# Gated DeltaNet heads in chunks of 128 with half-column inverse levels, and the transposes of v and k moved into the levels

## The chip, the cores and the metric

One Trainium2 chip, one of its cores. The metric is the device time of one execution in microseconds. The kernel before ran three times: 1482.9, 1483.9 and 1485.58 us, median 1483.9 us.

## The reference

One decoder layer on 512 tokens of width 1024, all in fp32. After an RMS norm, one projection feeds two mixers of 8 heads each. Mixer A is differential softmax attention. Mixer B is the gated delta rule: per head q, k, v (512 x 128, from a causal convolution, SiLU and, for q and k, an l2 norm), a decay g and a factor beta. The reference cuts the tokens into chunks of C = 64:

```python
A = jnp.eye(C, dtype=jnp.float32) + jnp.where(strict, kkT * decay, 0.0)
rhs = jnp.concatenate([v_beta, k_beta * jnp.exp(g)[..., None]], axis=-1)
sol = lax.linalg.triangular_solve(A, rhs, left_side=True, lower=True, unit_diagonal=True)
...
v_new = u_c - w_c @ state
o = (q_c * jnp.exp(g_c)[..., None]) @ state + a_c @ v_new
state = state * jnp.exp(g_last)[..., None, None] + jnp.swapaxes(k_dec, -1, -2) @ v_new
```

The result of the rule is the same for any chunk length, up to rounding. Behind the mixers come gates, an output projection, a gated MLP with a short convolution, and a gated embedding; none of that is touched.

## The kernel before

Tensors lie transposed, features on the 128 partitions and 512 tokens along the free dimension. A product with a weight matrix is a `gemm` (L470) of 8 contraction blocks. Each block is three matmuls of 512 columns (high and low halves of weights and activations). SP loads a chunk of weights, POOL (L420, L406) or ACT (L847) splits it.

Mixers A and B of all heads run in nine **turns**, h = -1 to 7. Turn h does head h of mixer B (`delta`) and head h+1 of mixer A (`attention`), and prepares qa and ka of head h+2. Turn -1 has no delta part, turn 7 has no attention part. Turns 0 to 5 are one loop. Below a turn is counted from its first product of kb with kb (L608), as turn 1 from 218.96 us.

Each engine has its order written by hand, with semaphores between them. TensorE has independent work to put between the dependent steps, the projections of the next head: `f.step(n)` issues n blocks of a gemm, three matmuls each, and `f.rest()` what is left. A loop turn has 7 gemms, so 56 steps.

On TensorE a turn runs so: scores of attention row block 0; 3 steps; the k-k and q-k products and the transposes of beta's columns (L608 to L616); 6 steps; the transpose of the softmax weights `pr` (L576), for which `combine` on DVE must be done; one step; the transpose of the first masked matrix `ct` (L625); scores; 5 steps; kb's transposes (L636). Then the inverse of the unit triangular matrix is built by doubling, in levels n = 1 to 5 over blocks of 2 to 64 tokens. `xi` holds the inverse so far, `xt` its transpose, for the four 128-token tiles:

```python
mm = pe.matmul(tiles(7)[:, t, :], ct[n % 2][:, t, :], xi[:, t, :], start=True, stop=True)
...
mm = pe.matmul(tiles(5)[:, t, :], xt[:, t, :], ui[:, t, :], start=True, stop=True)
...
mm = pe.matmul(tiles(6)[:, t, :], ui[:, t, :], xt[:, t, :], start=True, stop=True)
```

The first (L644, called u) is copied by ACT to `ui` (L971). The other two (L658, v, and L661, vt) are subtracted from `xi` and `xt` by DVE. Two steps lie between u and v, two behind vt. Level 1 also holds vb's transposes (L651). v(1) then waits until DVE has scaled them (`vbt`, L1357), together with kb's (`kbe`, `kdec`). ACT's queue between has the SiLU of vb, the softmax of row block 1 (L920), two operations for qa, and then the copy `ui` of level 1.

After level 5 come the products for w and u (L674, L677), 3 steps, and the recurrence over eight chunks of 64 tokens. Each chunk is two products with the state (L691, L692), a step, two products with `vnew` (L696, L697), a step. DVE makes `vnew` (L1399) and the new `state` (L1405) of each, and between them takes from a list `side` of 12 pieces the convolutions of the next head's qb and kb and their SiLU products. The last piece of kb's convolution is L1273; SiLU (ACT), square (ACT), the sum over partitions (`b_sum`, L590), the root (ACT) and L1307 follow it, then the decay matrix and the next turn's DVE work.

Turn 6 has four gemms to fill with and turn 7 nine.

Of the kernel before, what the change touches and what calls it, by code (L numbers as in the profile page):

```python
# [20 lines left out]
CH = 64  # L21
NC = T // CH
LEVELS = (1, 2, 4, 8, 16, 32)
# [3 lines left out]
KP = PLE // P  # L27
EPS = 1e-6
# [17 lines left out]
def constants():  # L46
# [102 lines left out]
def build(nc, x, p, w_in, attn_norm, qnorm_a, knorm_a, lam_a, subln_a, rel_bias, conv_b, a_log_b,  # L149
# [4 lines left out]
    with ctx:  # L154
# [299 lines left out]
        def _(pe):  # L454
# [87 lines left out]
            pe.matmul(bank[5][:, 96:128], half, gg, start=True, stop=True).then_inc(sem("g_sums"), 1)  # L542
# [49 lines left out]
            def turn(h, at, fill, delta=True, attention=True, more_a=True, steps=(3, 6, 5, 2, 2, 3)):  # L592
# [1027 lines left out]
```

## Time and profile before

| what | value |
|---|---|
| median of three runs | 1483.9 us |
| the profiled execution | 1483.94 us, span 1482.2 us |
| PE busy | 1375.8 us, 93% |
| DVE, ACT, POOL busy | 819.8, 502.2, 642.7 us |
| mean granted TensorE clock | 0.979 of full speed |
| a loop turn | 92.2 us |
| turns 6 and 7 | 79.7 and 84.7 us |

PE is the matmul part of TensorE, PEld its weight loads. Both run in parallel and matmuls overlap by their pipeline, so the distance between starts is the price of one, not its duration. An fp32 matmul stands in the rows as two passes, each with its own weight load: x8 is four matmuls, one for each token tile. The time in brackets behind a row is the engine's idle time before it and what ended it.

### The profile page before, as it was taken

To read this page: it belongs to the slowest core of one execution; us is meant where nothing else is said; L and a number is where in the kernel's file an instruction comes from. 1 tells how busy PE (TensorE), PEld (TensorE's weight loads), DVE (VectorE), ACT (ScalarE), POOL (GpSimd) and SP (SyncE) were. 2 spreads that over 40 slices of the span, in tenths; PEclk is the share of its full clock that TensorE was granted. 3 is DMA by queue.
4 is the path that set the end of the run, shared out by engine and by line. 5 is a ranking of instruction groups with operands and counts; after the bars stand their busy time and mean duration, and the time that the engine had idled before them with its cause. 6 is when DMAs were issued, how large, how long until landed. Compare 5 with 4: busy or idle time off the path is not lost.

```text
span 1482.2 us, 20910 instructions
## 1 busy us (share of the span) xinstructions
PE 1375.8 (93%) x6565; PEld 1065.9 (72%) x6565; DVE 819.8 (55%) x1305; ACT 502.2 (34%) x771; POOL 642.7 (43%) x757
## 2 busy tenths in 40 slices
PE   4887998989989899898889999999999999999998
PEld 3565766758667586676668688887887778888776
DVE  3256657575675756757674311321788883683633
ACT  4334344243332433323342242234432222222253
POOL 2352233232333322333224355644676766666543
PEclk9999999999999999999989999999999999999999
DMA  5321111111111111111101233422232333323223
GB/s 172 86 63 37 44 43 35 35 42 42 42 42 28 42 42 42 43 30 54 32 17 55 57 92 93 156 85 72 85 99 86 91 94 110 89 87 97 78 68 96
DMA packets 188101, 100.28 MB, mean 68 GB/s; under 512 B 3654, under 2 KB 186905, under 8 KB 188057
## 3 DMA queue, kind: packets, MB, share of 16 engines
q1 hardware_dynamic: 188057, 99.72, 23.4%
q8 instruction: 24, 0.39, 0.1%
q14 instruction: 20, 0.16, 0.0%
HBM read 97.60 MB, written 2.11 MB: 67 GB/s over the span
## 4 chain that ended last, share of the span: by engine, by line
PE 46%; POOL 18%; DVE 16%; issue 16%; ACT 2%; DMA 1%; DVEq 1%; SPq 1%; POOLq 0%; ACTq 0%
PE bank L470 26%; POOL w_lo L406 18%; PE bank L658 2%; PE bank L661 2%; PE bank L696 2%; PE bank L644 2%; PE bank L691 1%; DVE ast L1240 1%; PE bank L692 1%; PE bank L590 1%; PE bank L569 1%; PE bank L583 1%; DVE bank L1236 1%; DVE ct L1300 1%; DVE vb L1269 1%
## 5 line engine op out<-in xcount | busy, mean ns | idle before, releaser
L406 POOL TENSOR_TENSOR w_lo<-w_raw,w_hi 128x256 fp32r<-128x256 f32 x692 | 578.5, 868 | 303.4 <-ACT w_hi L847 298.5
L470 PE MATMUL bank<-hn_hi,w_hi 128*128 128x512 f32 x1000 | 421.7, 422 | 9.5 <-POOL w_lo L406 7.9
L470 PE MATMUL bank<-hn_hi,w_lo 128*128 128x512 f32 x1000 | 394.3, 394 | 0.0
L470 PE MATMUL bank<-hn_lo,w_hi 128*128 128x512 f32 x1000 | 393.4, 393 | 0.0
L420 POOL CAST w_hi<-w_raw 128x1024 fp32r<-128x1024 f32 x61 | 64.0, 1050 | 522.2 <-PE bank L470 522.2
L470 PEld LDWEIGHTS bank<-hn_hi,w_hi 128*128 128x128 f32 x1000 | 190.8, 191 | 54.2 <-issue 13.3
L470 PEld LDWEIGHTS bank<-hn_hi,w_lo 128*128 128x128 f32 x1000 | 189.7, 190 | 42.1
L470 PEld LDWEIGHTS bank<-hn_lo,w_hi 128*128 128x128 f32 x1000 | 190.5, 191 | 34.3 <-issue 3.4
L847 ACT ACTIVATE w_hi<-w_raw 128x1024 fp32r<-128x1024 f32 x120 | 127.4, 1062 | 198.7 <-PE bank L470 185.6
L1519 DVE SCALAR_TENSOR_TENSOR u<-vr,pt,u 128x511 f32<-128x511 f32 x88 | 75.7, 860 | 12.9 <-DVE u L1517 1.2
L470 PE MATMUL bank<-fa_hi,w_hi 128*128 128x512 f32 x176 | 71.3, 405 | 1.7 <-POOL w_lo L406 1.7
L470 PE MATMUL bank<-fa_hi,w_lo 128*128 128x512 f32 x176 | 68.6, 390 | 0.0
L470 PE MATMUL bank<-fa_lo,w_hi 128*128 128x512 f32 x176 | 68.6, 390 | 0.0
L1102 ACT ACTIVATE s<-u 128x512 f32<-128x512 f32 x22 | 13.9, 633 | 154.1 <-DVEq L1522 154.1
L1236 DVE TENSOR_TENSOR bank<-bank,bias 128x256 f32<-128x256 f32 (+1 forms) x64 | 25.6, 400 | 58.7 <-PE bank L569 52.2
L971 ACT ACTIVATE ui<-bank 128x512 f32<-128x512 f32 x40 | 23.9, 599 | 92.0 <-PE bank L644 90.5
L644 PEld LDWEIGHTS bank<-xi,ct 128*128 128x128 f32 x320 | 41.1, 193 | 18.4 <-issue 12.4
L658 PE MATMUL bank<-ui,xt 128*128 128x128 f32 x256 | 39.2, 302 | 13.4 <-DVE vbt L1357 13.4
L920 ACT ACTIVATE pr<-bank,ast 128x128 f32<-128x128 f32 (+3 forms) x64 | 33.8, 528 | 49.1 <-DVE ast L1241 47.7
L644 PE MATMUL bank<-xi,ct 128*128 128x128 f32 x320 | 44.3, 282 | 6.3 <-DVE xi L1347 6.3
L658 PEld LDWEIGHTS bank<-ui,xt 128*128 128x128 f32 x256 | 36.8, 212 | 17.4 <-DVE vbt L1357 15.3
L1399 DVE TENSOR_TENSOR vnew<-vbt,bank 64x128 f32<-64x128 f32 x64 | 18.3, 286 | 56.1 <-PE bank L691 52.9
(264 smaller groups left out, 2102.5 us busy)
## 6 DMA issues: line engine op xcount, KB each, us to landing
w_raw<-in_w_in SPq DMA_DIRECT2D x73, 512.0 KB, 3.7
w_raw<-in_w_up SPq DMA_DIRECT2D x44, 512.0 KB, 3.7
w_raw<-in_w_down SPq DMA_DIRECT2D x16, 512.0 KB, 3.5
w_raw<-in_w_br_a SPq DMA_DIRECT2D x8, 512.0 KB, 3.6
w_raw<-in_w_br_b SPq DMA_DIRECT2D x8, 512.0 KB, 3.6
w_raw<-in_w_out SPq DMA_DIRECT2D x8, 512.0 KB, 3.6
w_raw<-in_w_ple_gate SPq DMA_DIRECT2D x8, 512.0 KB, 3.6
w_raw<-in_w_down SPq DMA_DIRECT2D x8, 384.0 KB, 3.2
```

The costliest lines, as they stand in the source:

```text
L406: ins = pool.tensor_tensor(wlo[c.slot][:, ks, :], raw[c.slot][:, ks, :], whi[c.slot][:, ks, :].bitcast(F32), ALU.subtract)
L420: pool.tensor_copy(whi[c.slot][:, :, :], raw[c.slot][:, :, :]).then_inc(high_ready, 1)
L470: mm = pe.matmul(acc, w[c.slot][:, i, :], xx[:, x0 + i, :], start=(i == 0 and n == 0), stop=last)
L644: mm = pe.matmul(tiles(7)[:, t, :], ct[n % 2][:, t, :], xi[:, t, :], start=True, stop=True)
L658: mm = pe.matmul(tiles(5)[:, t, :], xt[:, t, :], ui[:, t, :], start=True, stop=True)
L661: mm = pe.matmul(tiles(6)[:, t, :], ui[:, t, :], xt[:, t, :], start=True, stop=True)
L696: pe.matmul(bank[7][:, 0:P], kdec[r, t, :], vnew[r, :], start=True, stop=True).then_inc(sem("kv"), 1)
L847: done(nc.scalar.activation(whi[c.slot][:, :, :], raw[c.slot][:, :, :], ACT.Copy), high_ready, c.number + 1)
L920: done(nc.scalar.activation(pr[j][:, 0:w], bank[3 + j][:, 0:w], ACT.Exp, bias=ast[:, 2 + j:3 + j], accum_out=ast[:, 4 + j:5 + j]), "a_exp" ...
L971: done(nc.scalar.activation(ui[:, :, :], tiles(7), ACT.Copy), "ui", h * 5 + n)
L1236: link(V.tensor_tensor(b[:, w - near:w], b[:, w - near:w], bias_of(h, near), ALU.add))
L1519: link(V.scalar_tensor_tensor(out=u[:, back:], in0=vr[:, 0:T - back], scalar=tap(j), in1=u[:, back:], op0=ALU.mult, op1=ALU.add))
```

## The change

Mixer B works in chunks of 128 tokens: the masks and the sums of g no longer stop at 64. The inverse needs a sixth level. In each level only half of the columns of `xi` and `xt` change, so v and vt take only these as the moving operand (`lane`, 64 of 128 columns in runs of m) and write them packed; DVE subtracts 256 instead of 512 columns. u stays whole. The recurrence has four chunks instead of eight; the first needs no product with the state, the last makes no new state.

The order changes too. On DVE the first `xt`, the second mask and the first `xi` go ahead of vb's convolution, `xt` also ahead of `combine`, and `qeg` goes into level 1, behind `combine` and vb's SiLU product. On TensorE vb's transposes go into level 2 and kb's into level 3, each with a wait in front of that level's v. The steps per turn are the same number: 15 ahead of level 1, 4 more in level 6, 8 instead of 16 in the recurrence and 4 at the end. The sum for qb's root (`b_sum(a, 0)`) goes behind them. Turn 6 spreads its steps thinner. On DVE three pieces of `side` go behind levels 5 and 6, seven into the recurrence, and the output of attention (`o_a`) behind the recurrence's last chunk. The constants that are loaded at the start grow from 12 to 13 blocks of 128 columns.

The diff, cut to its core and without the leading indentation:

```diff
-LEVELS = (1, 2, 4, 8, 16, 32)
+LEVELS = (1, 2, 4, 8, 16, 32, 64)
+NL = len(LEVELS)
...
+def lane(a, n, odd):
+    return a.rearrange("p (b two m) -> p b two m", two=2, m=LEVELS[n])[:, :, odd, :]
+def packed(b, n, t=None):
+    a = bank[b][:, 0:T // 2] if t is None else bank[b][:, t * 64:t * 64 + 64]
+    return a.rearrange("p (b m) -> p b m", m=LEVELS[n])
...
-    f.step(steps[1])
+    f.step(steps[1] - 1)
+    if delta:
...
+            mm = pe.transpose(tiles(7)[:, t, :], ct[0][:, t, :], ident)
...
+    f.step(2)
     if attention:
         turn_w(a, 0)
     f.step(1)
-    if delta:
...
-            mm = pe.transpose(tiles(7)[:, t, :], ct[0][:, t, :], ident)
...
-    f.step(steps[2])
-    if delta:
...
-            mm = pe.transpose(tiles(6)[:, t, :], kb[:, t * P:(t + 1) * P], ident)
-        mm.then_inc(sem("kb_T"), 1)
-    for n in range(1, 6):
+    f.step(steps[2] - 1)
+    for n in range(1, NL):
...
-        f.step(steps[3])
         if delta:
-            if n == 1:
+            if n == 2:
                 pe.wait_ge(sem("vb_ready"), h + 1)
...
+            if n == 3:
+                pe.wait_ge(sem("xt"), h * NL + n)
...
+                mm.then_inc(sem("kb_T"), 1)
+        f.step(steps[3])
+        if delta:
+            if n == 1:
+                pe.wait_ge(sem("qk_read"), h + 1)
+            if n == 2:
                 pe.wait_ge(sem("turned_read"), h + 1)
...
+            if n == 3:
+                pe.wait_ge(sem("kb_read"), h + 1)
...
-                    mm = pe.matmul(tiles(5)[:, t, :], xt[:, t, :], ui[:, t, :], start=True, stop=True)
+                    mm = pe.matmul(packed(5, n, t), xt[:, t, :], lane(ui[:, t, :], n, 0), start=True, stop=True)
...
-                mm = pe.matmul(tiles(6)[:, t, :], ui[:, t, :], xt[:, t, :], start=True, stop=True)
+                mm = pe.matmul(packed(6, n, t), ui[:, t, :], lane(xt[:, t, :], n, 1), start=True, stop=True)
...
-    for c in range(NC):
...
+    for t in range(NT):
+        ts = slice(t * P, (t + 1) * P)
+        v = us[:, 0, :] if t == 0 else vnew[:, :]
+        if delta and t > 0:
...
+            pe.matmul(bank[5][:, 0:P], wt_[:, t, :], state[:, :], start=True, stop=True).then_inc(sem("ws"), 1)
+            pe.matmul(bank[6][:, ts], state[:, :], qeg[:, t, :], start=True, stop=False, skip_group_check=True)
         f.step(1)
...
+            if t < NT - 1:
+                pe.matmul(bank[7][:, 0:P], kdec[:, t, :], v, start=True, stop=True).then_inc(sem("kv"), 1)
+            mm = pe.matmul(bank[6][:, ts], v, at_[:, t, :], start=(t == 0), stop=True, skip_group_check=True)
...
         f.step(1)
-        if c == 0 and attention:
+        if t == 0 and attention:
             attend(a)
-        if c == 2 and attention:
+        if t == 1 and attention:
...
-        if c == 6 and attention:
-            b_sum(a, 0)
     f.rest()
...
         mm.then_inc(sem("g_rows"), 1)
+        b_sum(a, 0)
         b_sum(a, 1)
...
-turn(H - 2, place(stream.late, LATE), fill_of(stream.late, LATE), more_a=False)
+turn(H - 2, place(stream.late, LATE), fill_of(stream.late, LATE), more_a=False, steps=(2, 4, 4, 1, 1, 2))
...
-    for n in range(1, 6):
+    for n in range(1, NL):
         if delta:
...
+                if n == 2:
+                    dve.wait_ge(sem("vb_T"), h + 1)
...
+                if n == 3:
+                    dve.wait_ge(sem("kb_T"), h + 1)
...
-                done(V.tensor_tensor(xi[:, :, :], xi[:, :, :], tiles(5), ALU.subtract), "xi", h * 5 + (n + 1))
+                done(V.tensor_tensor(lane(flat(xi), n, 0), lane(flat(xi), n, 0), packed(5, n), ALU.subtract),
+                     "xi", h * (NL - 1) + (n + 1))
...
+        if n == 1 and delta:
+            steps(finish_silu(h, 2))
+            link(V.tensor_tensor(flat(qeg), qb[:, :], flat(eg), ALU.mult))
...
+        if n >= 5 and attention and delta:
+            for _ in range(n - 4):
+                side.pop(0)()
...
-    for c in range(NC):
...
+    for t in range(NT):
+        if delta and t > 0:
+            dve.wait_ge(sem("ws"), h * 3 + t)
+            done(V.tensor_tensor(vnew[:, :], us[:, t, :], bank[5][:, 0:P], ALU.subtract), "vnew", h * 3 + t)
         if side:
             side.pop(0)()
...
-        if c == 1 and more_a:
+        if t == 0 and more_a:
             prep(h + 2, 1)
-        if c == 4 and attention:
...
-        if c in (1, 2, 3, 5, 6) and side:
+        elif side:
             side.pop(0)()
+    if attention:
+        dve.wait_ge(sem("oa_r"), a + 1)
...
     steps(side)
```

Two places in the order of the engines. First DVE, in a loop turn, from the operation behind the mask of level 0 (`ct0`) on. Before:

```order
L1333 TENSOR_TENSOR qeg<-qb,eg 128x512
L1147 REGISTER_ALU
L1249 REGISTER_ALU
L1250 RECIPROCAL ast<-ast 128x2
L1147 REGISTER_ALU
L1251 TENSOR_SCALAR ast<-ast,sm 128x1
L1147 REGISTER_ALU
L1252 TENSOR_SCALAR pr1<-pr1,ast 128x128
L1147 REGISTER_ALU
L1253 SCALAR_TENSOR_TENSOR pr0<-pr0,ast,pr1 128x128
L1337 TENSOR_TENSOR xt<-sq,ct0 128x512
L1300 TENSOR_TENSOR ct1<-lt,sq 128x512
```

The same place after the change:

```order
L1350 TENSOR_TENSOR xt<-sq,ct0 128x512
L1266 REGISTER_ALU
L1267 RECIPROCAL ast<-ast 128x2
L1164 REGISTER_ALU
L1268 TENSOR_SCALAR ast<-ast,sm 128x1
L1164 REGISTER_ALU
L1269 TENSOR_SCALAR pr1<-pr1,ast 128x128
L1164 REGISTER_ALU
L1270 SCALAR_TENSOR_TENSOR pr0<-pr0,ast,pr1 128x128
L1317 TENSOR_TENSOR ct1<-lt,sq 128x512
L1158 REGISTER_ALU
L1357 TENSOR_TENSOR xi<-sq,bank7 128x512
```

`xt` has taken the place of `qeg` ahead of the softmax combination (L1250 to L1253 before), and `xi` now follows the mask at once; before it stood behind vb's convolution.

Second TensorE, in a loop turn, from the attention product with va (L583) to the next. Before, from the end of that product on:

```order
L583 MATMUL bank<-wT,va 128x128
L690 REGISTER_ALU
L691 MATMUL bank<-state,ui 64x128
L692 MATMUL bank<-qeg,state 128x64
L470 MATMUL bank<-hn_hi,w_hi 128x512
L470 MATMUL bank<-hn_lo,w_hi 128x512
L470 MATMUL bank<-hn_hi,w_lo 128x512
L695 REGISTER_ALU
L696 MATMUL bank<-vnew,kdec 128x128
L697 MATMUL bank<-at_,vnew 128x64
```

After the change the same piece stands so:

```order
L591 MATMUL bank<-wT,va 128x128
L705 REGISTER_ALU
L706 MATMUL bank<-state,ui 128x128
L707 MATMUL bank<-qeg,state 128x128
L478 MATMUL bank<-hn_hi,w_hi 128x512
L478 MATMUL bank<-hn_lo,w_hi 128x512
L478 MATMUL bank<-hn_hi,w_lo 128x512
L715 MATMUL bank<-vnew,kdec 128x128
L716 MATMUL bank<-at_,vnew 128x128
```

The four products of a chunk are now whole 128 by 128 ones, and there are half as many chunks; the steps between them are as before.

## Rows read from the trace of the kernel before

**Rows 1.** The page's first part: busy time of each engine.

```profile
PE 1375.8 (93%) x6565; PEld 1065.9 (72%) x6565; DVE 819.8 (55%) x1305; ACT 502.2 (34%) x771; POOL 642.7 (43%) x757
```

**Rows 2.** Windows view of turns 1, 6 and 7: PE, PEld, DVE, ACT, POOL busy; clock; DMA.

```profile
218.96:311.17 92.21, 85.18 (x448) 63.27 (x447) 59.62 (x107) 34.06 (x64) 29.20 (x35) 0.98 0.15 40
679.85:759.52 79.67, 71.22 (x369) 52.99 (x370) 55.78 (x106) 28.70 (x55) 17.28 (x20) 0.91 0.12 34
759.52:844.17 84.65, 80.34 (x431) 63.61 (x430) 38.58 (x60) 21.81 (x35) 34.69 (x41) 0.98 0.18 50
```

**Rows 3.** Timeline of PE, turn 1: start, us, engine, line, shapes, [idle before].

```profile
227.05 0.33 PE L576 MATMUL bank<-sq,pr 128*128 128x128 f32 x1 [1.53 <-DVE pr L1253]
...
239.06 0.66 PE L651 MATMUL bank<-sq,vb 128*128 128x128 f32 x4 [1.92 <-DVE vb L1284]
241.56 2.08 PE L658 MATMUL bank<-ui,xt 128*128 128x128 f32 x8 [1.84 <-DVE vbt L1357]
```

**Rows 4.** Timeline of ACT, turn 1.

```profile
237.76 0.47 ACT L920 ACTIVATE pr<-bank,ast 128x256 f32<-128x256 f32 x1 [1.92 <-DVE ast L1241]
...
240.42 0.60 ACT L971 ACTIVATE ui<-bank 128x512 f32<-128x512 f32 x1
```

**Rows 5.** Timeline of DVE, turn 1.

```profile
224.15 0.69 DVE L1333 TENSOR_TENSOR qeg<-qb,eg 128x512 f32<-128x512 f32 x1
...
236.62 1.06 DVE L1241 TENSOR_SCALAR ast<-ast 128x2 f32<-128x2 f32 x1
```

**Rows 6.** Timeline of DVE, end of turn 1.

```profile
299.52 0.75 DVE L1273 SCALAR_TENSOR_TENSOR kb<-bank,pt,kb 128x509 f32<-128x509 f32 x1 [0.15 <-DVE vnew L1399]
...
308.30 0.83 DVE L1307 SCALAR_TENSOR_TENSOR kb<-kb,sqb 128x512 f32<-128x512 f32 x1 [0.30 <-ACT sqb L839]
```

**Rows 7.** Windows view, two short stretches, columns as in rows 2.

```profile
242.00:244.00 2.00, 2.00 (x11) 2.00 (x11) 0.56 (x2) 0.44 (x1) 0.00 (x0) 0.50 0.82 220
...
743.00:746.00 3.00, 2.81 (x10) 1.90 (x10) 2.54 (x5) 0.63 (x1) 0.00 (x0) 0.50 0.00 0
```

**Rows 8.** Timeline of PE: one whole level in turn 1.

```profile
259.98 1.05 PE L644 MATMUL bank<-xi,ct 128*128 128x128 f32 x8
260.79 0.47 PE L470 MATMUL bank<-hn_hi,w_hi 128*128 128x512 f32 x1
...
262.26 1.05 PE L658 MATMUL bank<-ui,xt 128*128 128x128 f32 x8
263.15 1.06 PE L661 MATMUL bank<-xt,ui 128*128 128x128 f32 x8
263.96 0.48 PE L470 MATMUL bank<-hn_hi,w_hi 128*128 128x512 f32 x1
```

**Rows 9.** Timeline of PE: chunks 5 and 6 of turn 1's recurrence, and 7's start.

```profile
295.64 0.43 PE L691 MATMUL bank<-state,ui 128*64 128x128 f32 x2
...
297.12 0.48 PE L696 MATMUL bank<-vnew,kdec 64*128 64x128 f32 x2
...
298.60 0.43 PE L691 MATMUL bank<-state,ui 128*64 128x128 f32 x2
...
302.42 0.43 PE L691 MATMUL bank<-state,ui 128*64 128x128 f32 x2
```

**Rows 10.** Timeline of PE and of its weight loads, chunk 0 of turn 1.

```profile
277.71 0.43 PE L691 MATMUL bank<-state,ui 128*64 128x128 f32 x2
278.07 0.43 PE L692 MATMUL bank<-qeg,state 128*128 128x64 f32 x2
278.07 0.30 PEld L692 LDWEIGHTS bank<-qeg,state 128*128 128x128 f32 x2 [0.17 <-issue]
```

**Rows 11.** Timeline of PE, turn 7, waits merged with their rows' starts.

```profile
776.62 1.67 PE L644 MATMUL bank<-xi,ct 128*128 128x128 f32 x8 [2.32 <-DVE xi L1347]
...
782.72 1.16 PE L658 MATMUL bank<-ui,xt 128*128 128x128 f32 x8 [0.85 <-DVE vbt L1357]
```

**Rows 12.** Waits view: the one wait of the ones-product of kb's and qb's squares.

```profile
PE bank L590 <- DVE o_a L1412: 4.9, 1, 4.9
```

More of the change, by code:

```diff
@@ L27 @@
 KP = PLE // P
+PIECE = 2
 EPS = 1e-6
@@ L56, in constants @@
     put(C_FLIP, j + i == P - 1)
-    put(C_CUM, same & (j <= i))
-    put(C_HALF, same)
+    put(C_CUM, j <= i)
+    put(C_HALF, j // HEAD == i // HEAD)
     put(C_ONES, np.ones((P, P)))
-    put(C_MASK, np.where(same & (j <= i), 0.0, NEG))
+    put(C_MASK, np.where(j <= i, 0.0, NEG))
     for n, m in enumerate(LEVELS):
@@ L541, in _ @@
             pe.matmul(bank[5][:, 64:96], cum, gg, start=True, stop=True)
-            pe.matmul(bank[5][:, 96:128], half, gg, start=True, stop=True).then_inc(sem("g_sums"), 1)
+            pe.matmul(bank[5][:, 96:128], ones, gg, start=True, stop=True).then_inc(sem("g_sums"), 1)
             def qk_sum(h, n, c):
@@ L693, in turn @@
                     f.step(1)
                     if delta:
-                        pe.wait_ge(sem("vnew"), h * 8 + (c + 1))
-                        pe.matmul(bank[7][:, 0:P], kdec[r, t, :], vnew[r, :], start=True, stop=True).then_inc(sem("kv"), 1)
-                        mm = pe.matmul(bank[6][:, cs], vnew[r, :], at_[r, t, r], start=False, stop=True, skip_group_check=True)
-                        if c == NC - 1:
+                        if t == 0:
+                            pe.wait_ge(sem("u_copied"), h + 1)
+                        else:
+                            pe.wait_ge(sem("vnew"), h * 3 + t)
@@ L1299, in make_ct @@
             def make_ct(h, n):
-                done(V.tensor_tensor(ct[n % 2][:, :, :], lt[:, :, :], level_mask(n), ALU.mult), "ct", h * 6 + (n + 1))
+                done(V.tensor_tensor(ct[n % 2][:, :, :], lt[:, :, :], level_mask(n), ALU.mult), "ct", h * NL + (n + 1))
             def head_start(h):
@@ L1332, in turn @@
                     make_ct(h, 0)
-                    link(V.tensor_tensor(flat(qeg), qb[:, :], flat(eg), ALU.mult))
+                    done(V.tensor_tensor(xt[:, :, :], ident.unsqueeze(1).to_broadcast([P, NT, P]), ct[0][:, :, :],
+                                         ALU.subtract), "xt", h * NL + 1)
                 if attention:
@@ L1400, in turn @@
+                for t in range(NT):
+                    if delta and t > 0:
+                        dve.wait_ge(sem("ws"), h * 3 + t)
+                        done(V.tensor_tensor(vnew[:, :], us[:, t, :], bank[5][:, 0:P], ALU.subtract), "vnew", h * 3 + t)
                     if side:
                         side.pop(0)()
-                    if delta:
-                        dve.wait_ge(sem("kv"), h * 8 + (c + 1))
-                        last = 64 * (c % 2) + 63
-                        done(V.scalar_tensor_tensor(out=state[:, :], in0=state[:, :], scalar=eg[:, t, last:last + 1],
-                                                    in1=bank[7][:, 0:P], op0=ALU.mult, op1=ALU.add),
-                             "state", h * 9 + (c + 2))
@@ L1417, in turn @@
+                    if t == 0 and more_a:
+                        prep(h + 2, 1)
+                    elif side:
+                        side.pop(0)()
+                if attention:
+                    dve.wait_ge(sem("oa_r"), a + 1)
+                    done(V.scalar_tensor_tensor(out=dyn(o_a, a),
+                                                in0=bank[3][:, :], scalar=gsub, in1=pr[1][:, :],
+                                                op0=ALU.mult, op1=ALU.mult), "oa_done", a + 2)
                 steps(side)
```

102 lines of the change are left out of this document (45 added, 57 removed).

## The prediction

> **What bounds the kernel.** I read the page's busy times first: TensorE is busy 93% of the span, the next engine 55% [rows 1]. Then the windows of single turns, because the change touches only the nine turns. A loop turn lasts 92.2 us and its matmuls are busy 85.2 of them, so some 7 us of it are waits; DVE is busy 59.6 us. Turn 6 has 71.2 of 79.7 busy at a mean clock of 0.91, turn 7 80.3 of 84.7 [rows 2]. All three kinds of turn are thus neither purely TensorE's nor purely another engine's, and the question is which stretch of a turn follows which engine.
>
> The waits of turn 1 answer it. They stand close together: 1.53 us ahead of the first softmax transpose, 1.92 ahead of vb's transposes, 1.84 ahead of v(1) [rows 3]. The page names vb and vbt for the last two, but ACT's queue stands beside them. The copy `ui` of level 1 ends at 240.42 + 0.60 = 241.02, and v(1) starts at 241.56. That copy is behind the softmax of row block 1, which started at 237.76, when DVE's last operation for it (236.62 + 1.06 = 237.68) was done [rows 4, 5]. So up to v(1) the turn follows a chain DVE, ACT, TensorE, and TensorE only fills. From v(1) on TensorE has no long wait, and its own work sets the pace. I call the start of v(1) V, and the end of the last piece of kb's convolution K: from K on DVE and ACT again make a chain to the next V. Turn 1: V = 241.56, K = 299.52 + 0.75 = 300.27 [rows 3, 6], so V to K is 58.7 us and K to the next V 92.2 - 58.7 = 33.5 us.
>
> One more thing is seen in the windows. Behind these waits the granted clock is 0.50, that is 1.2 instead of 2.4 GHz, from 242 to 244 us and, in turn 6, from 743 to 746 us where its recurrence runs without fill [rows 7]. In turn 1 it costs the eight passes of v(1) 2.08 us against 1.05 in level 4 [rows 3, 8]; with vt(1) I take 1.5 us per turn for it.
>
> **The change, part by part, in a loop turn.**
>
> Prices. In level 4 u takes 260.79 - 259.98 = 0.81 us, v 0.89, vt 0.81, and two steps 1.47, so 0.73 a step [rows 8]. A chunk takes 298.60 - 295.64 = 2.96 us, less two steps 1.49; the chunk with b_sum(a, 0) in it takes 302.42 - 298.60 = 3.82, so that sum costs 0.86 [rows 9].
>
> What does a product with 64 instead of 128 moving columns cost? The trace has both side by side. L691 moves 128 columns, L692 64, and both take 0.43 us for their two passes; a weight load of L692 follows the other by about 0.11 us (0.30 for two that last 0.19 each), which is 0.89 / 8 as in a level [rows 8, 10]. So I price a half-column product like a whole one: nothing is gained on TensorE. The bounds are this price and half of it, for eleven groups of v and vt 11 x 0.42 = 4.6 us per turn. I take the first because L692 is the same case. The Trainium skill, in "TensorE: Matmul & The Clock Gate", section "LDWEIGHTS (loading the stationary operand)", says that a load takes the number of columns over 1.2 in ns whatever the rows are; by that rule 128 columns take 107 ns and the halving is worth nothing, and the trace agrees with its 0.11 us.
>
> V to K. The end of this stretch is set by the recurrence's last chunk on TensorE: behind its `vnew` DVE still has qb's SiLU product, a piece of kb's convolution, `o_a` and the last piece. Before, the last chunk began at 302.42, V + 60.9, and K came a little ahead of it. Now, up to the last chunk: four steps fewer (-2.9); level 6 with u and vt, and a v in level 5 (0.81 + 0.81 + 0.89 = +2.5); the transposes of v and k, formerly ahead of V, at most 0.66 each [rows 3], of which I take 0.5 (+1.0); instead of seven chunks a half one and two whole ones, 10.4 to 3.7 (-6.7); b_sum(a, 0) moved behind (-0.9). New waits come in: vb's SiLU product now stands behind level 1's `combine`, so vb's transposes wait about 0.8 us, then v(2) 0.3 for vbt; v(3) waits for a mask, kbe and kdec (three of 0.69 us, the price of qeg [rows 5]) behind level 2's maxima, about 1.3 us. Together +2.4. The sum is -4.6, so the last chunk begins at V + 56.3. The DVE operations behind it are `vnew` (0.8 us after the start) and four of 0.7 to 0.8: K = V + 60.3 against 58.7, **+1.6 us**. The recurrence's saving is eaten by kb's convolution, which waits in DVE's queue behind it. The halved subtractions on DVE lie inside TensorE's steps and are worth nothing.
>
> K to V. `qeg` (0.69 us [rows 5]) leaves the chain, and v(1) no longer waits for vbt, 241.56 - 241.02 = 0.54. b_sum(a, 1) is no longer just behind its neighbour: L1307 had 0.30 idle ahead [rows 6]. Together **-1.5 us**. The earlier `xi` only moves the wait: u(1) comes about 2 us earlier and TensorE then stands some 5.5 us in one piece ahead of v(1), since `ui` is as late as ACT's softmax makes it. The low clock there stays, 1.5 us as before.
>
> So a loop turn changes by +0.1, six of them by +0.6. TensorE's work falls by some 4.5 us per turn, and its waits grow by as much.
>
> The other turns. Turn 7 has no attention, so no softmax ahead of `ui`. Its waits for xi (2.32) and vbt (0.85) [rows 11] go; the recurrence drops from 11.9 to 4.9 (half, two whole and three quarters of a chunk), the sixth level adds 2.5: -4.5 - 3.2, with 0.3 of the slow u behind the wait **-8**. Turn 6 is short of fill. Its thinner steps let the clock stay high in the recurrence, but the level waits (2.4 and 2.7 us where fewer steps cover them) and DVE's last pieces behind the recurrence cost about as much; I take **+1**, between -5 and +6. Turn -1 waits 4.9 us for o_a [rows 12], which now goes ahead of kb's SiLU product, but attention comes four steps (2.9 us) later; with 65 KB more of constants at the start **-1**.
>
> The sum is 0.6 - 8 + 1 - 1 = -7.4 us. The profiled execution took 1483.94, the same as the median; so 1476.5 us.
>
> **The rivals.**
>
> *TensorE sets the whole turn.* If the waits stay at 7 us instead of growing, the work taken away counts: 7 turns x -4.5 and turn 7's -8 give -40, 1444 us. For it speaks the busy share of 92% [rows 2]; against it that `ui` of level 1 is fixed by ACT's queue and K by DVE's. Halfway in between is as likely as the full effect, if kb's last pieces find their place earlier.
>
> *Half columns cost half.* 4.6 us for eight turns on top of the forecast: -37, 1440 us. The Trainium skill's section "Back-to-back issue gap" on the same page gives a gap that falls with the moving columns, which taken alone would make it so. L692's 0.43 us stands against it [rows 10].
>
> *Slower: one long wait and a low clock.* TensorE's wait ahead of v(1) is now in one piece, and more waits follow in levels 2 and 3, in front of each of which the matmuls stand behind. If the clock stays at 0.50 until v(3), not only for v(1) and vt(1), 5 us more of busy matmuls take twice as long, of which 2.5 lie on the path per turn. That is +15 for six turns and +4 in turn 6: 1476.5 + 19 = 1495. It decides if the low stretch in front of level 2 is over 3 us longer than today's [rows 7]. Half of it gives 1486, and that already is the other side.
>
> *Nothing moves.* Turn 7's saving may be lost in turn 6 (bound +6): within 3 us of 1483.9.
>
> **How the numbers follow.** My forecast has a chance of 0.55, with a range of its own of 1465 to 1487. TensorE's whole saving or half of it 0.17, half columns 0.06, slower 0.22. Three us, 0.2%, is what a measurement can tell from no change. Of the forecast's 0.55, 0.45 are faster by more than that, 0.08 within, 0.02 slower. So faster 0.45 + 0.17 + 0.06 = 0.68, same 0.08, slower 0.24. The range takes in half of the first rival and most of the slower one: 1450 to 1491.
>
> **What would show it.** A loop turn near 92 us; v and vt groups of eight passes still 0.8 to 0.9 us apart; one wait of over 4 us ahead of v(1), named after `ui` on ACT; short waits ahead of vb's transposes and of v(3); K about 60 us behind V, with DVE waiting for the recurrence's products before it; turn 7 at about 77 us. The forecast is wrong if v takes under 0.6 us, if a loop turn is under 90 us, or if the low clock lasts beyond level 1.

## The result, and the profile after

The changed kernel takes 1495.6 us (median of six runs, 1491.8 to 1499.4), the one before 1483.4 in the same series: ratio 1.0082, interval 1.0064 to 1.0101. It is slower by 12 us, where 1476.5 was forecast. The profiled execution took 1497.6 us with a span of 1495.5, and the mean granted clock fell from 0.979 to 0.944. Of all executions behind the medians of this document one stands apart, the first of e11 below, which took 1901.1 us at a mean clock of 0.654 and was the one profiled; without it e11's median is 1489.45 instead of 1490.5 us.

The page of the changed kernel, busy times; TensorE and DVE have less to do than before [rows 1]:

```profile
PE 1369.0 (92%) x6453; PEld 1089.6 (73%) x6453; DVE 783.0 (52%) x1241; ACT 506.7 (34%) x779; POOL 637.2 (43%) x757
```

Its windows of turns 2, 6 and 7. The columns are those of [rows 2]; the third number from the end is the granted clock:

```profile
320.61:416.24 95.63, 85.79 (x434) 67.49 (x433) 54.83 (x100) 34.61 (x64) 28.57 (x35) 0.89 0.14 38
...
702.14:782.49 80.35, 67.89 (x360) 51.26 (x358) 49.82 (x97) 29.74 (x57) 15.66 (x20) 0.91 0.10 27
...
782.49:857.21 74.72, 71.68 (x417) 61.57 (x416) 35.58 (x51) 21.38 (x34) 34.76 (x41) 1.00 0.20 55
```

Turns 0 to 5 now last 96.3, 95.8, 95.6, 95.6, 95.6 and 94.8 us, 573.6 together against 550.8: **+22.8**. Turn 6 is +0.7. Turn 7 ends with its last product with `ones` at 857.21, before at 844.17: 74.7 against 84.65 us, -9.9. The part ahead of the turns is 0.5 shorter. The sum is +13.0, the spans differ by 13.3. Though the instructions are fewer, 434 instead of 448, TensorE is busy a little longer in a loop turn than before, 85.8 against 85.2 us, and the clock is 0.89 instead of 0.98. So the whole loss lies in the loop turns. The matmuls' busy time does not fall with their number, because some of them are slow, and the time in which TensorE stands grew by 2.8 us, from 7.0 to 9.8 (window less PE busy).

TensorE's timeline in turn 2 of the changed kernel, the rows around the waits, in level 5 and at the end (start, us, engine, line, operands, idle time before and its cause):

```profile
341.17 1.94 PE L673 MATMUL bank<-ui,xt 128*128 128x64 f32 x8 [4.78 <-issue]
342.90 1.91 PE L676 MATMUL bank<-xt,ui 128*128 128x64 f32 x8
...
347.27 1.11 PE L647 MATMUL bank<-xi,ct 128*128 128x128 f32 x8
...
350.05 1.00 PE L673 MATMUL bank<-ui,xt 128*128 128x64 f32 x8
350.88 1.06 PE L676 MATMUL bank<-xt,ui 128*128 128x64 f32 x8
...
360.67 1.66 PE L673 MATMUL bank<-ui,xt 128*128 128x64 f32 x8 [1.75 <-DVE kdec L1383]
362.12 1.91 PE L676 MATMUL bank<-xt,ui 128*128 128x64 f32 x8
...
366.50 1.71 PE L647 MATMUL bank<-xi,ct 128*128 128x128 f32 x8
...
399.41 0.38 PE L706 MATMUL bank<-state,ui 128*128 128x128 f32 x2
...
407.86 1.15 PE L598 MATMUL bank<-sqb,sq 128*128 128x512 f32 x2 [1.97 <-ACT sqb L960]
409.87 2.08 PE L738 MATMUL bank<-sqo,sq 128*128 128x512 f32 x2 [0.86 <-ACT sqo L1034]
```

The same stretch in windows of three us, where the clock is low:

```profile
342.00:345.00 3.00, 3.00 (x15) 3.00 (x15) 0.50 (x2) 0.49 (x1) 0.00 (x0) 0.50 0.51 151
...
363.00:366.00 3.00, 3.00 (x10) 2.59 (x10) 1.64 (x5) 0.00 (x0) 0.00 (x0) 0.50 0.00 0
...
411.00:414.00 3.00, 2.98 (x9) 1.65 (x8) 2.24 (x5) 2.70 (x5) 0.00 (x0) 0.50 0.52 152
```

Three stretches at 0.50 (1.2 GHz) stand in a loop turn where one stood [rows 7]: behind the waits ahead of v(1), ahead of v(3) and at the turn's end. Level 2 between them is at full clock: v(2) and vt(2) take 0.83 and 0.87 us.

The other two engines behave as forecast. ACT's copy `ui` of level 1 still stands behind the softmax: it ends at 340.47 + 0.60 = 341.07, and v(1) starts 0.10 us later, though the profile names no engine for that wait ("issue"). The last piece of kb's convolution still stands on DVE behind the recurrence:

```profile
340.47 0.60 ACT L988 ACTIVATE ui<-bank 128x512 f32<-128x512 f32 x1
```

```profile
403.38 0.75 DVE L1290 SCALAR_TENSOR_TENSOR kb<-bank,pt,kb 128x509 f32<-128x509 f32 x1 [0.15 <-DVE o_a L1439]
```

So V = 341.17 and K = 404.13. V to K is 63.0 us (before 58.7, forecast 60.3), K to V 32.7 (33.5, 32.0).

### The profile page after: what moved, and what is told of

It is laid out like the page before. It is cut to its first block, busy times and chain, and to the rows that moved or that the text cites. A ratio compares the mean times of both kernels' runs of the same rounds, so it can differ in the third digit from the quotient of the medians.

```text
span 1495.5 us, 20470 instructions
## 1 busy us (share of the span) xinstructions
PE 1369.0 (92%) x6453; PEld 1089.6 (73%) x6453; DVE 783.0 (52%) x1241; ACT 506.7 (34%) x779; POOL 637.2 (43%) x757
## 4 chain that ended last, share of the span: by engine, by line
PE 48%; POOL 18%; issue 17%; DVE 12%; ACT 3%; DMA 1%; SPq 1%; DVEq 0%; POOLq 0%; ACTq 0%
PE bank L478 28%; POOL w_lo L414 18%; PE bank L676 3%; PE bank L673 3%; PE bank L647 2%; PE bank L577 2%; DVE ct L1317 1%; DVE ast L1257 1%; PE bank L591 1%; PE bank L738 1%; DVE bank L1253 1%; PE bank L584 1%; DVE pr L1269 1%; PE bank L555 0%; PE bank L616 0%
## 5 line engine op out<-in xcount | busy, mean ns | idle before, releaser
L414 POOL TENSOR_TENSOR w_lo<-w_raw,w_hi 128x256 fp32r<-128x256 f32 x692 | 573.6, 860 | 303.8 <-ACT w_hi L864 298.9
L478 PE MATMUL bank<-hn_hi,w_hi 128*128 128x512 f32 x1000 | 429.7, 430 | 10.6 <-POOL w_lo L414 9.2
L478 PE MATMUL bank<-hn_hi,w_lo 128*128 128x512 f32 x1000 | 403.7, 404 | 0.0
L478 PE MATMUL bank<-hn_lo,w_hi 128*128 128x512 f32 x1000 | 402.5, 403 | 0.0
L478 PEld LDWEIGHTS bank<-hn_lo,w_hi 128*128 128x128 f32 x1000 | 197.0, 197 | 36.0 <-issue 2.9
L673 PE MATMUL bank<-ui,xt 128*128 128x64 f32 x320 | 49.7, 306 | 47.0 <-issue 32.6
L673 PEld LDWEIGHTS bank<-ui,xt 128*128 128x128 f32 x320 | 47.5, 222 | 56.7 <-issue 35.3
L647 PEld LDWEIGHTS bank<-xi,ct 128*128 128x128 f32 x384 | 56.5, 215 | 16.1 <-issue 8.7
L676 PE MATMUL bank<-xt,ui 128*128 128x64 f32 x384 | 62.0, 315 | 0.0
L1386 DVE TENSOR_TENSOR xi<-xi,bank 128x256 f32<-128x256 f32 x40 | 16.8, 421 | 82.7 <-PE bank L673 81.9
L676 PEld LDWEIGHTS bank<-xt,ui 128*128 128x128 f32 x384 | 58.7, 231 | 1.1 <-ACT ui L988 0.5
L1253 DVE TENSOR_TENSOR bank<-bank,bias 128x256 f32<-128x256 f32 (+1 forms) x64 | 25.5, 399 | 62.3 <-PE bank L577 55.1
```

Of the source, the lines that this page charges most:

```text
L414: ins = pool.tensor_tensor(wlo[c.slot][:, ks, :], raw[c.slot][:, ks, :], whi[c.slot][:, ks, :].bitcast(F32), ALU.subtract)
L478: mm = pe.matmul(acc, w[c.slot][:, i, :], xx[:, x0 + i, :], start=(i == 0 and n == 0), stop=last)
L673: mm = pe.matmul(packed(5, n, t), xt[:, t, :], lane(ui[:, t, :], n, 0), start=True, stop=True)
L676: mm = pe.matmul(packed(6, n, t), ui[:, t, :], lane(xt[:, t, :], n, 1), start=True, stop=True)
L1253: link(V.tensor_tensor(b[:, w - near:w], b[:, w - near:w], bias_of(h, near), ALU.add))
L1386: done(V.tensor_tensor(lane(flat(xi), n, 0), lane(flat(xi), n, 0), packed(5, n), ALU.subtract), "xi", h * (NL - 1) + (n + 1))
```

## The experiments

All times are medians; each ratio is to the kernel before in the same series. That kernel gave 1483.2 to 1483.8 us in the four series. The traces are of one execution each. Theory A puts the loss on the clock, theory B on the new order of work.

**e1, e2: TensorE kept busy in its waits.** `warm(n)` issues n 512-column products that nobody reads:

```diff
+def warm(n):
+    for _ in range(n):
+        pe.matmul(bank[5][:, :], hn_hi[:, 0, 0:P], hn_hi[:, 0, :], start=True, stop=True)
...
 if n == 1:
+    if attention:
+        warm(18)
     pe.wait_ge(sem("qk_read"), h + 1)
```

> The changed kernel with extra 512-column products on TensorE whose result nothing reads, put where TensorE stands still: 18 ahead of v(1), 6 ahead of v(3), 8 ahead of the second b_sum and 3 ahead of the ob sum (0.23 us each, so 4.1, 1.4, 1.8 and 0.7 us, inside waits of 4.8, 1.75, 2.0 and 0.9 us). They add work and take nothing away. Theory A, the clock: the three stretches at 0.50 go, v(1) with vt(1) takes 1.7 instead of 3.4 us, v(3) likewise, the start of the next turn is no longer slow; a loop turn falls from 95.7 to about 91.5 us, the kernel to 1470 (1465 to 1476). Theory B, the order of work (DVE's chain to kb's last piece): the clock rises but a loop turn stays within 1 us, 1490 to 1496. If the extra products get in the way it is above 1496.

> Only the 18 extra products ahead of v(1). Theory A: this stretch of low clock alone costs v(1), vt(1) and two steps 1.7 + 1.2 us, so about 2.9 us per loop turn if nothing behind absorbs it: 1495.6 - 6 x 2.9 - 2 (turn 6) = 1476. If v(3) waits longer as v(1) comes through faster, it is half of that, 1486. Theory B: 1493 to 1496.

e1 took 1455.2 us (0.9821, 0.9793 to 0.9849), 40 us less than the changed kernel although it does more. A loop turn of e1:

```profile
309.91:399.23 89.32, 85.54 (x469) 67.11 (x469) 54.55 (x100) 34.68 (x65) 28.70 (x35) 1.00 0.15 41
```

It lasts 89.3 instead of 95.6 us at clock 1.00, more than the 4 us I expected. (The profiled execution took 1466.6 us, 11 above the median; its loop turns last 89.2 to 90.9.) V to K is 58.1 us (330.48 to 388.58), K to V 31.2. The starts of v in the loop turns show where the six us are, in the mean of six turns: v(1) to v(2) 7.09 instead of 8.93 us, v(3) to v(4) 5.55 instead of 8.77, and K to V, in turn 2, 31.2 instead of 32.7. These are 1.8, 3.2 and 1.5 us. At v(1) the slow products had lost more, 2.8 us by the distance to u(2), but TensorE now waits for vb's SiLU product in level 2. e2, with the first wait alone filled, took 1470.2 (0.9905, 0.9875 to 0.9935), a loop turn 92.3, less than either value I had for theory A. So the first wait is worth a little over half of the six us, but not by the first stretch alone: v(1) to v(2) is 1.8 us shorter, and v(3) to v(4) 1.6 in turn 2 (7.13 against 8.76), because the slow stretch behind v(3) is shorter too, its wait being the same 1.74 us. K to V stays at 32.6 to 32.7. Theory B as put for these two runs is refuted.

**e3: real work in the long wait.** Five fill steps from behind vt in levels 2 to 6 go between u(1) and v(1), in the loop turns:

```diff
-f.step(steps[3])
+f.step(steps[3] + (5 if n == 1 and delta and more_a else 0))
...
-f.step(steps[4])
+f.step(steps[4] - (1 if n > 1 and delta and more_a else 0))
```

> Five fill steps moved in the six loop turns, none added: one taken from behind vt in each of the levels 2 to 6, all five put between u(1) and v(1), where TensorE stands 4.8 us. 5 x 0.7 = 3.5 us leave the stretch from V to K, and the wait ahead of v(1) falls to about 1.3 us. Theory A: 3.5 us from the steps and 2 to 3 us from the clock per loop turn, so -5.5 x 6: 1463 (1458 to 1475). Theory B, K is set by DVE's chain and the level's latency rather than by TensorE's work: only the part beyond it shows, the levels wait longer instead: 1488 to 1496.

1458.5 us (0.9833, 0.9793 to 0.9874), 37 us less, by theory A. The wait ahead of v(1) is 1.40 us and v(1) is at full clock. Some low clock is left. It is at the turn's end in turns 0 to 2. In turns 0 and 1 it is also at v(2), where v(2) to u(3) is 6.9 us instead of 5.4, and in turns 3 to 5 behind v(3), where v(3) to v(4) is 6.45 instead of 4.86. The waits ahead of v(2) and v(3) are only 1.0 to 1.1 us here.

**e4: whole columns.** The half columns are undone:

```diff
-mm = pe.matmul(packed(5, n, t), xt[:, t, :], lane(ui[:, t, :], n, 0), start=True, stop=True)
+mm = pe.matmul(tiles(5)[:, t, :], xt[:, t, :], ui[:, t, :], start=True, stop=True)
...
-mm = pe.matmul(packed(6, n, t), ui[:, t, :], lane(xt[:, t, :], n, 1), start=True, stop=True)
+mm = pe.matmul(tiles(6)[:, t, :], ui[:, t, :], xt[:, t, :], start=True, stop=True)
```

> The half columns undone: v and vt move 128 columns again, DVE subtracts 512 instead of 256 columns (0.69 instead of 0.42 us), all else as in the changed kernel. If a half-column product costs the same as a whole one (0.83 against 0.89 us per group of eight passes at full clock): within 3 us of 1495.6, at most +0.06 x 11 x 7 = +4.6 where TensorE sets the pace. If the halving is worth half a product: +4.6 us a turn, 1527. In slow stretches v(1) with vt(1) should take about the same 3.4 us.

This was the surprise: 1478.4 us (0.9976, 0.9961 to 0.999), 17 us less, with twice the columns to move. TensorE at v(1) and v(3) in turn 2 of e4:

```profile
335.00 2.05 PE L673 MATMUL bank<-ui,xt 128*128 128x128 f32 x8 [4.79 <-issue]
...
341.07 1.05 PE L647 MATMUL bank<-xi,ct 128*128 128x128 f32 x8
...
354.86 1.16 PE L673 MATMUL bank<-ui,xt 128*128 128x128 f32 x8 [1.74 <-DVE kdec L1383]
355.85 1.06 PE L676 MATMUL bank<-xt,ui 128*128 128x128 f32 x8
...
358.14 1.05 PE L647 MATMUL bank<-xi,ct 128*128 128x128 f32 x8
```

At v(3) the wait is the same, 1.74 us, but the clock stays up: v(3) to u(4) is 3.28 us instead of 366.50 - 360.67 = 5.83. What lies between these starts is the same everywhere, v, vt and two steps, so I read both distances in every loop turn (0 to 5) of several traces:

| kernel | v(1) to u(2), us | v(3) to u(4), us |
|---|---|---|
| before (64 chunks, whole columns) | 3.27, 4.70, 4.66, 4.64, 4.62, 4.64 | 3.17 or 3.18 in all |
| e6: before with half columns | 5.92, 4.34, 5.84, 4.48, 6.14, 5.97 | 3.17 or 3.18 in all |
| changed (half columns) | 5.96, 6.11, 6.10, 6.11, 6.12, 6.11 | 5.39, 5.73, 5.83, 5.89, 5.89, 5.88 |
| e4: changed, whole columns | 4.87, 4.72, 6.07, 4.77, 6.08, 4.77 | 3.28 or 3.29 in all |
| e5: whole in level 3 only | 5.99, 6.11, 6.10, 6.06, 5.77, 6.11 | 3.27 or 3.28 in all |
| e15: half in level 3 only | 4.87, 4.82, 6.11, 4.86, 6.11, 4.85 | 4.77, 5.56, 3.27, 5.54, 3.29, 5.56 |

At full clock the first is 3.27 (turn 0 of before, where the clock did not fall). Half columns make the stretch at v(1) long in nearly every turn, whole ones in two of six; at v(3) only half columns bring one. The means of the changed kernel are 6.09 and 5.77, of e4 5.21 and 3.28. The loop turns differ by 3.3 us (573.6 against 554.0 for six), and that is v(3) alone. From v(3) to v(4) the changed kernel takes 8.77 us in the mean, e4 5.55. From v(1) to v(2) both take the same, 8.93 and 8.96: where the stretch at v(1) is short, TensorE waits for vb's SiLU product instead.

The turn's end can be read in e4 alone. Turns 2 and 4 end at clock 1.00, and K to V is 31.2 us in both; turn 3 ends with a stretch at 0.50, and it is 32.6:

```profile
404.00:406.00 2.00, 2.00 (x10) 1.57 (x10) 1.40 (x5) 1.37 (x3) 0.00 (x0) 1.00 0.00 0
...
496.00:498.00 2.00, 2.00 (x6) 1.55 (x5) 1.51 (x4) 1.23 (x2) 0.00 (x0) 0.50 0.00 0
```

**e5, e11, e15: one level alone.** e5 has whole columns in level 3 only; e11 and e15, the same kernel twice, have half columns in level 3 only:

```diff
-mm = pe.matmul(packed(5, n, t), xt[:, t, :], lane(ui[:, t, :], n, 0), start=True, stop=True)
+if n == 3:  # e11, e15: n != 3
+    mm = pe.matmul(tiles(5)[:, t, :], xt[:, t, :], ui[:, t, :], start=True, stop=True)
+else:
+    mm = pe.matmul(packed(5, n, t), xt[:, t, :], lane(ui[:, t, :], n, 0), start=True, stop=True)
```

> The changed kernel with whole columns (and whole subtractions) in level 3 alone, half columns everywhere else. Run e4 (whole columns in every level) took 1478.4 us and showed no low clock behind the 1.74 us wait ahead of v(3), where the changed kernel has 0.50. Theory A: the 64-column products directly behind that wait let the clock fall, at this one place, so this run is as fast as e4: 1478 (1475 to 1482), v(3) with vt(3) 2.0 instead of 3.1 us. Theory B: half columns cost a little in every level: a sixth of e4's gain, 1492.

> The converse of e5: whole columns everywhere, half columns in level 3 alone. Theory A (the half-column products directly behind the 1.74 us wait ahead of v(3) let the clock fall): the low stretch at v(3) comes back and with it the whole loss, 1495 (1490 to 1498) against e4's 1478.4. Theory B (a little in every level): 1481.

> Kernel e11 once more (half columns in level 3 alone: 1490.5 us, with a profile that could not be read). Theory A wants v(3) with vt(3) at 3.1 us and a granted clock of 0.50 behind the wait for kdec, as in the changed kernel, and a time of 1488 to 1496. Theory B wants 2.0 us at clock 1.00.

e5 took 1475.3 us (0.9934, 0.9914 to 0.9954): level 3 gives the whole loss back. Its v(3) to v(4) is 5.56 us. DVE's subtractions are whole in this level too, but they come behind v(3), which in the changed kernel is slow itself (1.66 us in turn 2, in e4 1.16). The converse gave 1490.5 both times (1.004, 1.0019 to 1.0061, and 1.0047, 1.003 to 1.0063), some 12 us above e4. Its trace says why not 17 (v(3) to v(4) is 7.42 us in the mean, 1.87 above e4, six times of which is 11). TensorE at v(3) in two neighbouring turns of e15:

```profile
358.43 1.10 PE L676 MATMUL bank<-ui,xt 128*128 128x64 f32 x8 [1.74 <-DVE kdec L1389]
359.37 1.06 PE L682 MATMUL bank<-xt,ui 128*128 128x64 f32 x8
361.70 1.05 PE L647 MATMUL bank<-xi,ct 128*128 128x128 f32 x8
...
449.84 1.37 PE L676 MATMUL bank<-ui,xt 128*128 128x64 f32 x8 [1.74 <-DVE kdec L1389]
451.00 1.92 PE L682 MATMUL bank<-xt,ui 128*128 128x64 f32 x8
...
455.38 1.91 PE L647 MATMUL bank<-xi,ct 128*128 128x128 f32 x8
```

The clock behind them:

```profile
360.00:363.00 3.00, 3.00 (x20) 2.71 (x20) 2.20 (x6) 0.21 (x1) 0.00 (x0) 1.00 0.00 0
...
453.00:456.00 3.00, 3.00 (x9) 2.42 (x9) 2.54 (x6) 0.00 (x0) 0.00 (x0) 0.50 0.00 0
```

The instructions and the wait are the same. In one turn the clock stays up, in the next it falls, and the turns last 93.2, 96.1, 91.5, 96.2, 91.6 and 95.3 us. By the table it falls at v(3) in the four turns whose stretch at v(1) was short, and not in the two where it was long. In the changed kernel both are slow in all six.

**e6: half columns in the kernel before**, nothing else:

> The kernel before (chunks of 64, old order) with half columns in its levels and nothing else. Theory A: with waits of 1.5 to 1.9 us ahead of level 1, the low stretch at v(1) becomes longer and the steps behind it slower: +0.5 to +2 us per loop turn, 1487 to 1497. If half columns cost only where a wait of 1.75 us stands directly ahead of a full-clock stretch, and v(1) is slow already: 1482 to 1485. If halving saves anything: below 1481.

1490.4 us (1.0059, 1.0033 to 1.0085), +7 us. By the table v(1) to u(2) is 5.45 us in the mean against 4.42, six times 1.0. Two of its turns:

```profile
223.68:315.03 91.35, 85.33 (x448) 63.11 (x447) 56.42 (x107) 34.03 (x64) 29.08 (x35) 0.98 0.15 40
315.03:408.14 93.11, 86.33 (x447) 64.18 (x447) 57.23 (x107) 34.02 (x64) 29.18 (x35) 0.96 0.14 39
```

So the halving alone costs time in the old kernel too: its turn 2, with 5.84 us there, lasts 93.1, and turn 1, with 4.34, lasts 91.4, which is 0.9 less than before. In its profiled execution (1493.6 us) the loop turns are 6.4 us longer together, 3.9 of them in turn 0, where the kernel before has no low stretch at all; turn 6 is 2.6 longer.

**e7, e10: the order.** Both have chunks of 128 and whole columns. e7 has the whole old order ahead of the levels. e10 keeps of the new one the masks, `xt` and `xi` ahead of `combine` and `qeg` in level 1. In both vb's and kb's transposes are back:

```diff
+pe.wait_ge(sem("qk_read"), h + 1)
+for t in range(NT):
+    mm = pe.transpose(tiles(6)[:, t, :], kb[:, t * P:(t + 1) * P], ident)
+mm.then_inc(sem("kb_T"), 1)
...
-if n == 2:
-    pe.wait_ge(sem("vb_ready"), h + 1)
...
-if n == 3:
-    pe.wait_ge(sem("xt"), h * NL + n)
```

> Chunks of 128 with whole columns and the old order ahead of the levels: kb's transposes ahead of level 1, vb's in level 1, kbe, kdec and vbt made ahead of the levels, qeg and combine ahead of xt. Compared with e4 (1478.4 us: whole columns, new order) it prices the new order, compared with before (1483.8) the chunk change. Theory A: the wait ahead of v(1) is in pieces again and v(3) has none, one low stretch of about 2 us; but 2 to 3 us of DVE work are back in the chain ahead of V. By TensorE's time from V to K (kb's transposes 0.4, waits 2.3 less) and from K to V (+1.5) it is 1472 (1464 to 1480). If the order of the masks was the gain in e4: 1485 or more.

> Whole columns; of the new order only the first masks, xt and xi ahead of the softmax combination and qeg in level 1; vb's and kb's transposes, kbe, kdec and vbt stay at their old place ahead of v(1). It stands between e7 (1454.0, all old) and e4 (1478.4, all new). If the transposes in levels 2 and 3 carry the loss (their waits of 1.74 and 0.2 us lie where TensorE otherwise does not wait): 1452 to 1458. If the one long wait ahead of v(1) carries it: 1470 or more, since the earlier u(1) brings that wait together here too, though split by vb's transposes.

e7: 1454.0 us (0.979, 0.9754 to 0.9827). e10: 1449.2 (0.9762, 0.972 to 0.9805), 3 below my range. So the new chunks with the old order ahead of the levels win 29 us over the kernel before; in the profiled execution, 24 us below the one before, 12 lie in the six loop turns, 7 in turn 7 and 5.5 in turn 6, whose thinner steps e7 keeps. The masks bring about 5 more by the medians, with intervals that overlap. Moving the transposes into the levels, with DVE's work on them, from e10 to e4, loses 29. A loop turn of e10, and its v(1):

```profile
305.00:393.71 88.71, 81.34 (x434) 63.70 (x433) 57.54 (x100) 34.66 (x64) 28.63 (x35) 0.94 0.15 41
```

```profile
323.14 0.66 PE L661 MATMUL bank<-sq,vb 128*128 128x128 f32 x4 [1.92 <-DVE vb L1297]
...
325.63 2.08 PE L669 MATMUL bank<-ui,xt 128*128 128x128 f32 x8 [1.84 <-DVE vbt L1369]
327.50 1.60 PE L672 MATMUL bank<-xt,ui 128*128 128x128 f32 x8
330.34 1.05 PE L652 MATMUL bank<-xi,ct 128*128 128x128 f32 x8
```

The traces of e10 and e4 account for the 29: six loop turns 23.2, turn 6 5.4 (80.8 against 75.4), turn 7 0.6. In V to K, 55.7 against 60.3 us, stand 0.7 for the two groups of transposes, 1.9 for the new waits (1.74 and 0.18), and 1.4 for the longer low stretch at v(1), 6.07 against 4.71 us to u(2). In the turns of e4 where that stretch is short, TensorE waits 0.84 us for vb's SiLU product instead, so most of the 1.4 is lost there too. The remaining 0.7 of V to K is not attributed. K to V gives 0.5 to 1.8 back in turns 1 to 4. My expectation for e7, 1472, took no account of turn 6, 74.2 instead of 79.7 us.

**e8, e9, e14: a better version.** e8 is e3 with whole columns and the last four steps of a turn in its last waits. e9 is e7 with steps in its waits, e14 the same for e10. The diff of e9 against e7, beside e3's second line:

```diff
-f.step(steps[1])
+f.step(steps[1] + (1 if delta and more_a else 0))
...
-f.step(steps[3])
+f.step(steps[3] + (2 if n == 1 and delta and more_a else 0))
...
 mm.then_inc(sem("vb_T"), 1)
+if more_a:
+    f.step(2)
...
 b_sum(a, 0)
+f.step(3)
 b_sum(a, 1)
+f.rest()
```

> The changed kernel with whole columns, the five fill steps of e3 between u(1) and v(1), and the four steps left at the end of a turn moved into the two waits there (three ahead of the second b_sum, one ahead of the ob sum). Theory A: e3's 1458.5 less the low stretch at the turn's end, 1.5 to 2 us in each of six loop turns, and a little at v(3): 1447 (1440 to 1454), clock 0.98 or more in the loop turns. Theory B, the rest is DVE's chain: 1457 to 1460.

> Run e7 (chunks of 128, whole columns, old order: 1454.0 us) with fill steps moved in the loop turns: one ahead of the first softmax transposes, two ahead of vb's transposes and two behind them (waits of 1.5, 1.9 and 1.7 us), taken one by one from behind vt in levels 2 to 6, and the four last steps of a turn moved into the two waits at its end. Theory A: the low clock at v(1) and at the turn's end goes and V to K loses up to 5 x 0.7 us, of which DVE's chain lets about 1 us through: 1454 - 6 x 2.5 = 1439 (1432 to 1446), clock 0.99. Theory B, the turn already follows DVE's chain: 1451 to 1456 whatever the clock.

> Run e10 (1449.2 us: new masks, old transposes, whole columns, a loop turn of 88.7 us at clock 0.94) with the fill steps moved as in e9 (three ahead of vb's transposes, two behind them, one fewer behind each vt in levels 2 to 6) and the last steps of a turn in its two last waits. The masks were worth 5 us between e7 and e10. If they keep that: 1421. If with the clock at 1.00 the turn follows DVE's chain in either order: 1425 to 1430, as e9.

e8: 1456.1 us (0.9807, 0.9762 to 0.9851), no better than e3, a miss. Its loop turns have clock 1.00 and last 88.4 us against e3's 88.9: there was little left to win at the turn's end, where K to V was already 31.2 us in most turns of e3 and is 31.1 here, and TensorE waits 1.2 us for ACT's square of kb all the same. e9: 1425.4 (0.9601, 0.9559 to 0.9644), better than I expected. **e14: 1415.7 (0.9541, 0.9511 to 0.9572)**, 68 us below the kernel before and 80 below the changed one. A loop turn of e9 and of e14:

```profile
296.34:380.60 84.26, 77.67 (x433) 60.57 (x433) 58.60 (x100) 34.65 (x65) 29.95 (x35) 1.00 0.16 44
```

```profile
294.97:378.00 83.03, 77.51 (x433) 60.42 (x433) 58.59 (x100) 34.65 (x65) 30.39 (x35) 1.00 0.16 44
```

In e14 the masks keep their gain, 1.2 us a turn, though one step also stands elsewhere than in e9: it is ahead of vb's transposes and not of the first softmax transposes.

**e12, e13: what half columns are worth when the clock stays up.** e12 is e1 with whole columns, e13 is e9 with half columns:

> Run e1 (extra products in the waits, clock 1.00 in loop turns, 1455.2 us) with whole columns. With the clock held up on both sides only the bare price of half columns is left: at 0.83 against 0.89 us a group and 0.42 against 0.69 us on DVE, 1455 to 1460, e1 faster by 0 to 5 us. If half columns cost something besides the clock: below 1453.

> Run e9 (1425.4 us, clock 1.00 in the loop turns, no wait of TensorE over 1.04 us ahead of a level's v) with half columns in all levels. If half columns cost only where a longer wait stands ahead of them: the clock stays 1.00 and the bare saving shows, 0.5 us per loop turn as between e1 and e12, 1422 (1419 to 1426). If they let the clock fall by themselves: 1435 or more.

e12: 1463.2 us (0.9844, 0.98 to 0.9889), 3 above my range. e13: 1421.9 (0.9585, 0.9555 to 0.9616). By the medians half columns save 8 and 3.5 us, with intervals that overlap in both pairs. The loop turns are steadier: 89.3 (e1) against 89.9 (e12), 83.6 (e13) against 84.3 (e9). A turn of e12:

```profile
310.28:400.12 89.84, 85.49 (x469) 67.13 (x468) 57.51 (x100) 34.67 (x65) 28.69 (x35) 1.00 0.15 41
```

And one of e13:

```profile
295.63:379.24 83.61, 77.47 (x434) 60.60 (x433) 54.47 (x100) 34.66 (x65) 29.87 (x35) 1.00 0.16 44
```

So half columns do not lower the clock by themselves: in e13, with real work in its waits, it is 1.00 in the loop, and they are worth 0.6 us a turn.

## Why the prediction was wrong

Two sentences failed. The one that cost the time is "So I price a half-column product like a whole one: nothing is gained on TensorE". Its durations were right: a group at full clock takes 0.83 against 0.89 us. The Trainium skill's rule in "TensorE: Matmul & The Clock Gate", section "LDWEIGHTS (loading the stationary operand)", by which a load takes its columns over 1.2 in ns whatever the rows are (an estimate of 107 ns for 128 columns), is borne out within 3%: 0.83 / 8 is 0.104 us. But the price was taken at full clock only. In the sum, level 3 has its wait (1.3 us, measured 1.74) and nothing for a low clock behind it. Behind that wait a stretch at 0.50 followed with half columns and none with whole ones: 3.2 us from v(3) to v(4) in each loop turn, 17 us in all (e4; 20 by e5). So V to K came out at 63.0 us instead of 60.3, and the loop turns at +22.8 instead of +0.6.

The other is "The low clock there stays, 1.5 us as before". For before it is 1.4 (4.65 less 3.27 us). In the changed kernel the stretch at v(1) costs its own products 2.8 us (6.1 less 3.27), of which 1.8 reach v(2) (e1, e2), and a stretch at the turn's end adds some 1.5 us to K to V. These two also stand in e4, in part.

With whole columns the forecast's sums come out step by step, which is what the price "like a whole one" meant:

- V to K: forecast 60.3, e4 60.3 (335.00 to 395.33). Last chunk at V + 56.3, e4 V + 55.6.
- K to V: forecast 32.0, e4 between 31.2 and 33.0.
- A loop turn: forecast 92.3, mean of e4 92.3. Turn 6: +1, e4 +1.1. Turn 7: -8, measured -9.9 (e4 -9.7).
- The time: 1476.5, e4 1478.4.

That e4 comes out so near owes much to errors that cancel. The new waits with the transposes were put at 3.4 us and measured 2.6, while the low clock at v(1) was longer in two turns of six. The last chunk began 0.7 us earlier than forecast and K came 0.7 later behind it. And the low stretch at the turn's end, in four turns of six, was in no term.

Of the rivals, "Slower: one long wait and a low clock" gave 1495, the time that came. Its mechanism was half right. One long wait there is, and v(1) and v(3) are slow, but the clock does not stay low from v(1) to v(3): level 2 runs at full clock, and v(3) has a wait and a stretch of its own. I gave it 0.22. That its number came is in part luck: it had +16 for the six loop turns and +5 for turn 6, and they measured +22.8 and +0.7, with turn 7 at -9.9 instead of -8. The rival "TensorE sets the whole turn", 1444, failed as argued: K follows DVE's queue behind the recurrence, and the new waits grew. The rival "Half columns cost half" failed too: 0.6 us per turn at full clock, not 4.6. The forecast's own check "if the low clock lasts beyond level 1" was the right one to name, and the rows had what was needed to weight it more: the waits of 5.5 and 1.3 us that I wrote down myself, beside [rows 3, 7], where waits of 1.8 to 1.9 us already brought the clock to 0.50.

What the runs show: the loss at v(3) by an edit to that level alone (e5), that at v(1) by filling its wait (e2), that of the transposes from e10 to e4. The turn's end has no edit of its own; its price is read from e4's turns with and without the stretch. What is not shown: by what the chip decides when the clock falls, and why v(3) was spared in e15 behind a long stretch at v(1). Nor is it shown what about the half columns matters. They differ from whole ones in number and also in how they are read and written, in runs of m and packed, and no run has one without the other.

## What to carry to other kernels

Price a wait on TensorE twice, once as idle time and once as the slow products behind it, and ask of each wait that a change merges or creates whether work can be put into it: here the same instructions in another place were worth 34 us (e10 to e14). An edit that only makes products cheaper can lengthen the time if they stand behind a wait. And try the parts of a change singly: this one held a gain of 29 us (chunks), one of about 5 (masks, by the medians), a loss of 29 (transposes in the levels) and one of 17 (half columns).

## What was not expected of the hardware

Extra products that nobody reads made the kernel 40 us faster (e1). Behind the same wait of 1.74 us the clock fell behind 64-column products and stayed at 1.00 behind 128-column products (e4, e5), and in one kernel it did both, in neighbouring turns (e15). In the kernel before, halving the columns of nine groups in each turn cost 7 us (e6).
